# Up weights of the looped experts: one transfer of 16 KB rows per matrix in place of two of 8 KB rows

## The reference, cut to what matters

```python
for e in range(N_EXPERTS):                      # 32
    hid = silu(t @ w_up1[e]) * (t @ w_up3[e])   # w_up1[e], w_up3[e]: 1024 x 512
    y = y + combine[:, e:e + 1] * (hid @ w_down[e])   # w_down[e]: 512 x 1024
```

## Time and profile before

| | |
|---|---|
| runs | 1097.51, 1099.11, 1099.91 us; median 1099.11 us |
| span of the profiled execution | 1095.7 us (first to last instruction) |
| expert stage | from about 602 us of the span to about 1078 us |
| tail after the last expert | 17.7 us |

### The profile page before, as it was taken

How to read it: one execution, slowest core, us unless ns; L and a number is a source line. 1 busy time by engine, 2 the same in 40 slices (tenths; PEclk the granted TensorE clock), 3 DMA queues, 4 the chain that set the end, 5 groups by cost and what they waited for, 6 DMA issues and landing times.

```text
span 1095.7 us, 18202 instructions
## 1 busy us (share of the span) xinstructions
PE 1028.6 (94%) x7403; PEld 591.1 (54%) x7403; DVE 665.0 (61%) x1131; ACT 326.2 (30%) x500; POOL 167.4 (15%) x220
## 2 busy tenths in 40 slices
PE   3999999999999999999998999999999999889895
PEld 1588588755557677768884444444334333333332
DVE  2478768444457443238347777777776665666666
ACT  4342462366652223365351111111111101110114
POOL 0100000322220011264500200000000000001003
PEclk9999999999999999999999999999999999999998
DMA  9676303205320004243439999999999999999994
GB/s 342 245 242 217 136 28 127 77 13 180 115 77 2 3 4 157 72 155 123 172 122 407 376 396 401 400 402 399 407 404 408 404 404 395 405 396 402 411 423 196
DMA packets 67732, 275.22 MB, mean 251 GB/s; under 512 B 7742, under 2 KB 17256, under 8 KB 43098
## 3 DMA queue, kind: packets, MB, share of 16 engines
q1 hardware_dynamic: 62976, 263.84, 62.4%
q10 hardware_dynamic: 2218, 6.52, 1.6%
q0 software_dynamic: 2480, 4.01, 1.3%
HBM read 274.26 MB, written 4.21 MB: 254 GB/s over the span
## 4 chain that ended last, share of the span: by engine, by line
PE 45%; SPq 25%; DVE 13%; DMA 7%; ACT 5%; issue 3%; POOL 1%; DVEq 0%; ACTq 0%
SPq L476 17%; PE ps L2211 8%; SPq L480 5%; PE ps L2230 4%; PE ps L1878 3%; DMA ring<-in_w_in 3%; DMA arena<-in_w_up 2%; SPq L484 2%; PE ps L2195 2%; PE ps L1859 2%; DMA arena<-in_w_mod 2%; PE ps L1867 2%; PE ps L1979 2%; PE ps L1860 1%; PE ps L1861 1%
## 5 line engine op out<-in xcount | busy, mean ns | idle before, releaser
L1544 DVE TENSOR_TENSOR arena<-arena,ps 128x1024 f32<-128x1024 f32 x124 | 145.5, 1215 | 52.9 <-PE ps L2195 52.9
L2211 PE MATMUL ps<-arena 128*64 128x512 f32 x672 | 152.9, 596 | 12.0 <-DMA arena<-in_w_up 11.2
L2211 PEld LDWEIGHTS ps<-arena 128*64 128x64 f32 x672 | 47.5, 137 | 105.5 <-issue 99.8
L1054 ACT ACTIVATE results<-ps,ST 64x512 fp32r<-64x512 f32 x64 | 43.8, 685 | 182.8 <-PE ps L2230 182.4
L2211 PE MATMUL ps<-ring,arena 128*64 128x512 f32 x352 | 79.9, 597 | 6.9 <-DMA ring<-in_w_up 5.5
L1047 ACT ACTIVATE arena<-ps 128x256 f32<-128x256 f32 x32 | 12.3, 385 | 234.7 <-PE ps L2211 234.7
L1720 PE MATMUL ps<-h_upper,w_upper 128*128 128x512 f32 (+1 forms) x184 | 73.7, 401 | 4.8 <-POOL h_lower_first L604 4.6
L2230 PE MATMUL ps<-arena 128*64 128x512 f32 x336 | 76.7, 598 | 1.3 <-DMA arena<-in_w_down 1.3
L1554 DVE SCALAR_TENSOR_TENSOR results<-ps,ST,results 64x512 fp32r<-64x512 f32 x64 | 48.0, 749 | 47.4 <-ACT results L1054 46.9
L2195 PE MATMUL ps<-results,back 128*128 128x512 f32 x248 | 73.7, 419 | 0.0
L1722 PE MATMUL ps<-h_upper,w_lower 128*128 128x512 f32 (+1 forms) x184 | 72.1, 392 | 0.0
(11 more groups left out here) (424 smaller groups left out, 1866.7 us busy)
## 6 DMA issues: line engine op xcount, KB each, us to landing
arena<-in_w_up SPq DMA_DIRECT2D x84, 1024.0 KB, 28.1
ring<-in_w_up SPq DMA_DIRECT2D x44, 1024.0 KB, 27.7
ring<-in_w_down SPq DMA_DIRECT2D x11, 2048.0 KB, 32.4
arena<-in_w_down SPq DMA_DIRECT2D x11, 2048.0 KB, 31.4
arena<-in_w_down SPq DMA_DIRECT2D x20, 1024.0 KB, 27.2
ring<-in_w_mod SPq DMA_DIRECT2D x6, 2048.0 KB, 9.1
arena<-in_w_mod SPq DMA_DIRECT2D x6, 2048.0 KB, 9.5
ring<-in_w_in SPq DMA_DIRECT2D x6, 2048.0 KB, 8.4
```

The costliest lines, as they stand in the source:

```text
L1544: TT(two_banks(acc[:, t, :]), two_banks(acc[:, t, :]), ps[:, BACK_BANK[t]:BACK_BANK[t] + 2, :], ALU.add).then_inc(back_added, 1)
L2211: last = mm(ps[64 * hf:64 * hf + 64, UP_BANK, :].rearrange("p (m n) -> p m n", m=2), hgT[:, k, :], up_pair(u, k)[:, :, 256 * hf:256 * hf + ...
```

## The change

For experts 3 to 29, and for further blocks, SP no longer waits for `up_half`. It waits for `up_done` and then issues each up matrix whole, in one transfer of 2 MiB: one row of 16 KB for each partition, to the same place as the two halves before. Both transfers of an expert raise `w_in_sem[u][0]`, by 32 in all, as the two first halves did. PE waits for this semaphore ahead of the first step, so for both whole matrices, and waits for `w_in_sem[u][1]` only for experts 0 to 2 (`halves=1`) and 30 and 31 (`halves=2`), which are still loaded in halves. `up_half` is still signalled and used for experts 30 and 31. The down loads, the gathers and all work of the other engines stay.

```diff
+        def load_up(eng, u, e):
+
+            for i in range(2):
+                src = esrc[i][:, bass.ds(e, 1), :].rearrange("p a n -> p (a n)")
+                eng.dma_start(eset_up[u][i], src).then_inc(w_in_sem[u][0], 16)
+
...
             with sp.Fori(0, LOOPED // NSET - 1) as it:
                 for u in range(NSET):
-                    sp.wait_ge(up_half, NSET * it + (u + 1))
-                    load_expert(sp, u, 0, NSET * it + (NSET + u))
                     sp.wait_ge(up_done, NSET * it + (u + 1))
-                    load_expert(sp, u, 1, NSET * it + (NSET + u))
+                    load_up(sp, u, NSET * it + (NSET + u))
                     sp.wait_ge(down_done, NSET * it + (u + 1))
                     load_expert(sp, u, 2, NSET * it + (NSET + u))
...
-                        sp.wait_ge(up_half, NSET * it + (LOOPED + u + 1 - NSET))
-                        load_expert(sp, u, 0, e)
                         sp.wait_ge(up_done, NSET * it + (LOOPED + u + 1 - NSET))
-                        load_expert(sp, u, 1, e)
+                        load_up(sp, u, e)
...
-            def expert_up(u, it, before):
+            def expert_up(u, it, before, halves):
                 pe.wait_ge(hg_ready, NSET * it + (u + 1))
                 pe.wait_ge(w_in_sem[u][0], it * 32 + 32)
...
-                        pe.wait_ge(w_in_sem[u][1], it * 32 + 32)
+                        if halves:
+                            pe.wait_ge(w_in_sem[u][1], 32 * halves)
...
-            def expert(u, turn, before, last=False):
+            def expert(u, turn, before, last=False, halves=None):
 
-                expert_up(u, turn, before)
+                expert_up(u, turn, before, halves)
...
             for u in range(NSET):
-                expert(u, 0, u if u else None)
+                expert(u, 0, u if u else None, halves=1)
...
-            expert(0, again + 1, NSET * again + NSET)
-            expert(1, again + 1, NSET * again + (NSET + 1), last=True)
+            expert(0, again + 1, NSET * again + NSET, halves=2)
+            expert(1, again + 1, NSET * again + (NSET + 1), last=True, halves=2)
```

## The result

The changed kernel took 1103.09 us in the median of nine runs (1101.43 to 1106.23), the kernel before 1099.01 beside it (1096.89 to 1101.05): a ratio of 1.0044 with an interval of 1.0033 to 1.0056, so 4.8 us slower (3.6 to 6.2). The forecast was 1095.8 us, within 1093.0 to 1102.5: the sign was wrong.

A forecast was written before the change was run, and what follows sets the result against it. It took the continuous weight stream, from about 573 to 1073 us, to bound the kernel. Packets -4.6 and late first issue +1.3 gave -3.3 us: median from 1099.1 to 1095.8, range 1093.0 to 1102.5.

The forecast's parts named there:

- the coarser wait: PE starts an expert when 4 MiB have landed, not 2; costed at nothing, with 27 us of stream still ahead.
- PE's floor: Expert 31 could start at 1039.2 at PE's unstalled pace, so up to 24.2 us could be won before PE binds.
- The packets' saving: On up weight loads, 16 KB packets save fixed cost: 0.173 us an expert over 27 experts, taken as 4.6 us.
- I keep this price: In the weight stream, each expert's gather still costs 0.63 us, unchanged by longer packets.
- the mild form of rival B: Dips at gathers grow; doubled, 17 us, 1113; decides from 0.12 us a dip; a third of B's 0.16.
- The late first issue: In the loop's first turn SP issues only after `up_done`, near 609.2; loss 0 to 2.8 us, taken as 1.3.
- The 34.4 us of waits for up weights: PE's waits for up weights, 17.6 + 16.8 us, all placed in the stage's second half.
- A, unmerged: Up rows still travel as 8 KB, or the saving drowns; only the late issue remains, +1.3, 1100.4; chance 0.21.
- B in its strong form: On the DMA engines 16 KB weight packets take 1.14 us each: 225 us more, 1324; two thirds of B's 0.16.
- C: Stream runs dry behind PE's wait for whole matrices: up to +97 us, or 3.6 a turn; chance 0.04.
- D: A fixed cost per transfer is on the path: gain up to PE's floor, 24 us, 1075; chance 0.02.

The follow-up runs named there:

- the last turn alone: The kernel before, with only experts 27 to 29 loaded and awaited whole: 1101.69 us, ratio 1.0031.
- the wait alone: The kernel before, loads unchanged, with PE waiting for both up halves ahead of the first step for experts 3 to 29: 1102.69 us, ratio 1.0030.
- the last two runs: The kernel before with whole loads and waits in one turn only: experts 3 to 5, 1099.98 us, ratio 1.0010; experts 27 to 29, 1101.69 us, ratio 1.0031.

## Why the prediction was wrong

*The bound was read rightly for most of the stage, and wrongly for its end.* "The end moves by what the continuous weight stream ... gains or loses" held while PE had slack behind the last landing. The failed step is in the part on the coarser wait: "The last two experts keep halves, so the end from landing to last product stays as it is." It looked only at whether the stream would run dry, and it didn't. It left out that PE itself needs 14.1 us an expert. Once expert 29 may not start before all its up weights are there, PE has three experts to do: 42.7 us from their landing at 1042.94 to 1085.66. The stream needs 34.8 us for what is behind that landing (to 1077.7), and in the kernel before the end came 4.7 us behind it, 39.5 in all. The difference is 3.2 us; the last turn alone measured 3.4 us, the wait alone 3.3. The trace of before held its sign, if not its size: three experts are 42.4 us, against the prediction's own 36 us for those 14.7 MB and the 4.7 behind them, so 1.7 us. PE's floor was worked out for the whole stage, 24 us away, and not for its last three experts. For earlier turns the price is nothing that can be measured, as forecast, since PE wins 15.9 - 14.1 us back with each expert that follows.

The Trainium skill, Perfetto Trace Analysis, DMA Optimizations, says that splitting transfers may let some start sooner; the prediction named it and set it aside because the queue was full. The runs agree with it for one turn of nine, by 3.4 us, although the DMA engines were as busy there as before (421 GB/s from 1043 to 1077.7).

*The packets' saving was sized rightly for a stream alone, and taken whole for one that gathers share.* This is the second step that failed, and it costs the sum as much as the first: of the 4.6 us, 27 times 0.17, the streams beside gathers show 27 times 0.04, 1.1 us. The step is "I keep this price", 0.63 us a gather. The price was wrong for 8 KB packets already, where it came to 1.0: it set all bytes that moved, 378 against 422 GB/s, and so counted the gather's own 0.11 MB as weights, where SP's queue alone moved 2.16 MB of 2.53, 0.88 us; and a window of 6 us around a gather doesn't hold all that it slows. That alone would not have moved the sum. But the price rose by 0.13 us an expert, some 0.12 a gather, beside longer packets, and the prediction had this as the mild form of rival B, with 0.12 us a dip as the point from which it decides; that point was reached. Why a gather costs more beside long packets isn't shown. It lands later, from 700 to 1000 in the kernel before and in the changed kernel:

```profile
DMA to landing us min/median/max: 6.8/7.1/7.8
```

```profile
DMA to landing us min/median/max: 7.1/8.6/9.4
```

The Trainium skill, DMA: Bandwidth & Descriptors, Queues, rings and completion order, says that an engine drains a whole packet of one queue before it switches to another. By that a gather's packets would wait longer behind longer packets; the landings go that way, but no run tests it.

*The late first issue* was priced at 1.3 us and measured 1.1 (0.1 to 2.1) with whole rows; with halves nothing showed, and the two intervals overlap. That the middle of 0 to 2.8 was hit is luck as much as reading: the dents have 0.4 to 0.5 us of free time. Before the last two runs the differences of the others had put this turn at 1.9 and 2.5 us; with scatter of about a us in each ratio the three don't exclude each other.

*The sum* with what was measured is -1.1 + 1.1 + 3.4 = 3.4 us, against 4.8 (3.6 to 6.2) for the changed kernel; the rest lies within the intervals of the terms.

*A reading.* The 34.4 us of waits for up weights add those of PE and of its weight loads, which stand at the same landings. PE's idle time from 842 to 1068 is 226 - 206.66 = 19.3 us. No term of the sum used the 34.4.

*Rivals.* A, unmerged, is refuted by the packet count. B in its strong form is refuted: without gathers the longer packets are faster. C named a wait that bites, but by a dry queue; at the landing of expert 29's up weights 34.8 us of stream were still to come. D is refuted as a large term: without gathers all that was saved is 0.16 us an expert, about what the packets alone were to save.

No version tried beats the kernel before by more than its measurement can tell. The one with both outer turns in halves is level with it.

## What to carry to other kernels

When a stage is bound by a transfer queue, work out the end by both clocks: from the last few landings the stream needs so long and the engine behind it so long, and a wait made coarser costs where the engine's time is the longer. A stall that costs nothing in the middle, because the engine catches up, is paid in full when too few steps are left to catch up. And a saving per packet is worth what is left after the traffic that shares the engines; price that traffic from the whole period, not from the dip, and by the bytes of the stream that you want, not by all bytes.

## What the runs showed of the hardware

Two things were not expected. A gather of some 0.1 MB takes about 1.0 us from a stream that moves 0.42 MB in that time: by far more than its bytes. Without the gathers the kernel is 24 us faster, and then bound by PE, at the floor that the prediction had worked out (24.2 us).

The other is the clock. The coarse wait gathers PE's idle time of an expert in one piece, and behind such a piece the granted clock often fell for a short time. PE's timeline in the changed kernel, and stretches around it:

```profile
947.11 5.35 PE L2214 MATMUL ps<-arena 128*64 128x512 f32 x16 [2.25 <-DMA arena<-in_w_up]
```

```profile
940.00:948.00 8.00, 5.75 (x27) 2.22 (x29) 6.20 (x13) 1.36 (x2) 0.00 (x0) 1.00 1.00 393
948.00:952.00 4.00, 4.00 (x14) 1.36 (x10) 0.00 (x0) 0.00 (x0) 1.27 (x3) 0.57 1.04 438
```

After waits of 1.53 and 2.25 us for two experts in a row, four steps took 5.35 us where 3.65 are usual, at 0.57 of the full clock, mostly its lower level of 1.2 GHz. Here the stream set the pace and PE made it good. Five of the six profiles with coarse waits in these turns have this fall between 944 and 948, and the kernel before has none; the sixth, with both outer turns in halves, had waits of 2.06 and 2.35 us and no fall. In the last three experts, where PE sets the end, a fall costs time. The run with the first turn in halves had one in expert 28, which then took so long that expert 29 started without a wait, and PE ended 9.0 us behind the last landing in place of 7.9:

```profile
1025.71 5.35 PE L2223 MATMUL ps<-arena 128*64 128x512 f32 x16 [2.56 <-DMA arena<-in_w_up]
...
1041.59 3.60 PE L2223 MATMUL ps<-arena 128*64 128x512 f32 x16
```

In the changed kernel the same wait of 2.56 us in expert 28 had no fall behind it.
